# Eight weight buffers in SBUF, 1040 columns apart in place of 1024, the lower four moved by 4 columns

## The reference

```
mod = silu(c) @ w_ada + b_ada                 # 2048 x 12288, for 9 condition rows
h   = rmsnorm(x) * (1 + scale1) + shift1
qa, ka, va, qb, kb, vb, r, glr = split(h @ w_in)          # 2048 x 6160
x   = x + gate1 * (concat(attention, gated linear attention) @ w_out)   # 2048 x 2048
h2  = rmsnorm(x) * (1 + scale2) + shift2
g_pre, u = split(h2 @ w_up)                               # 2048 x 11264
x   = x + gate2 * ((silu(causal_conv(g_pre)) * u) @ w_down)             # 5632 x 2048
```

## Time and profile before

| what | value |
|---|---|
| time before, median of 3 runs | 1544.93 us (1543.18 to 1546.24) |
| profiled execution: span from first to last instruction | 1544.0 us |
| PE busy with matmuls | 1514.8 us, 98% of the span |
| PE loading stationary operands | 1372.8 us, 89% |
| DVE busy | 875.7 us, 57% |
| ACT busy | 633.9 us, 41% |
| matmuls of each of L989, L990, L991 | 3136 |

### The profile page before, as it was taken

One profiled execution on the slowest core, in us unless ns is written; L12 is line 12 of the kernel. 1 busy time (PEld: TensorE's weight loads), 2 busy tenths in 40 slices (PEclk: granted clock), 3 DMA queues, 4 the chain that ended last, 5 costly groups with the idle time before them and its releaser, 6 DMA issues.

```text
span 1544.0 us, 27862 instructions
## 1 busy us (share of the span) xinstructions
PE 1514.8 (98%) x11762; PEld 1372.8 (89%) x11762; DVE 875.7 (57%) x1509; ACT 633.9 (41%) x873; POOL 52.4 (3%) x89
## 2 busy tenths in 40 slices
PE   8999999999999889999999999999999999999999
PEld 4877888888888557768899999999999999999999
DVE  3655676666667435557454555555554565656574
ACT  3433444434445215235333333334333445545453
POOL 2000000001111000000000000000000000000000
PEclk8999999999999999999999999999999999999999
DMA  9998777777777997997644444454545444454541
GB/s 354 400 355 346 307 257 257 257 259 267 255 288 270 413 414 309 422 363 292 251 164 164 164 164 169 159 184 147 188 146 182 163 172 178 166 181 172 178 176 53
DMA packets 62283, 370.98 MB, mean 240 GB/s; under 512 B 7431, under 2 KB 7913, under 8 KB 27081
## 3 DMA queue, kind: packets, MB, share of 16 engines
q1 hardware_dynamic: 56096, 351.08, 60.6%
q0 software_dynamic: 5904, 17.93, 3.4%
q10 hardware_dynamic: 162, 0.22, 0.0%
HBM read 359.32 MB, written 9.88 MB: 239 GB/s over the span
## 4 chain that ended last, share of the span: by engine, by line
PE 89%; DMA 5%; DVE 3%; SPq 2%; ACT 1%; issue 1%; POOL 0%; ACTq 0%; DVEq 0%
PE ps L989 26%; PE ps L990 25%; PE ps L991 25%; PE ps L941 4%; PE ps L934 1%; SPq L710 1%; DMA ring<-in_w_ada_early 1%; DMA ring<-in_w_out 1%; DMA ring<-in_cache_k_win 1%; DMA proj<-in_tables 1%; ACT whi L1501 1%; DVE wlo L2028 1%; PE ps L1321 1%; DMA ring<-in_w_ada 1%; PE ps L1290 1%
## 5 line engine op out<-in xcount | busy, mean ns | idle before, releaser
L989 PE MATMUL ps<-hhi,whi 128*128 128x288 f32 x3136 | 934.0, 298 | 3.1 <-DVE wlo L1871 1.6
L990 PE MATMUL ps<-hlo,whi 128*128 128x288 f32 x3136 | 922.6, 294 | 0.0
L991 PE MATMUL ps<-hhi,wlo 128*128 128x288 f32 x3136 | 922.5, 294 | 0.0
L989 PEld LDWEIGHTS ps<-hhi,whi 128*128 128x128 f32 x3136 | 589.0, 188 | 38.8 <-issue 29.9
L990 PEld LDWEIGHTS ps<-hlo,whi 128*128 128x128 f32 x3136 | 589.2, 188 | 0.7
L991 PEld LDWEIGHTS ps<-hhi,wlo 128*128 128x128 f32 x3136 | 588.9, 188 | 0.0
L1492 ACT ACTIVATE whi<-ring 128x1024 fp32r<-128x1024 f32 x178 | 185.7, 1060 | 200.7 <-PE ps L991 200.7
L1864 DVE TENSOR_TENSOR wlo<-ring,whi 128x1024 fp32r<-128x1024 f32 x178 | 212.0, 1221 | 78.8 <-ACT whi L1492 78.4
L2028 DVE TENSOR_TENSOR wlo<-ring,whi 128x1024 fp32r<-128x1024 f32 x96 | 117.0, 1223 | 79.6 <-ACT whi L1501 79.5
L1501 ACT ACTIVATE whi<-ring 128x1024 fp32r<-128x1024 f32 x96 | 100.8, 1053 | 130.1 <-PE ps L991 114.2
L2545 DVE TENSOR_TENSOR wlo<-ring,whi 128x1024 fp32r<-128x1024 f32 (+1 forms) x94 | 105.7, 1132 | 56.2 <-ACT whi L1805 56.2
(11 more groups left out here) (298 smaller groups left out, 905.4 us busy)
## 6 DMA issues: line engine op xcount, KB each, us to landing
ring<-in_w_up SPq DMA_DIRECT2D x88, 1024.0 KB, 4.8
ring<-in_w_down SPq DMA_DIRECT2D x32, 1408.0 KB, 6.1
ring<-in_w_ada SPq DMA_DIRECT2D x42, 1024.0 KB, 6.8
ring<-in_w_in SPq DMA_DIRECT2D x28, 1024.0 KB, 6.5
ring<-in_w_ada_early SPq DMA_DIRECT2D x22, 1024.0 KB, 7.5
proj<-in_w_ada SPq DMA_DIRECT2D x22, 1024.0 KB, 11.0
ring<-in_w_in_early SPq DMA_DIRECT2D x20, 1024.0 KB, 9.3
ring<-in_w_out SPq DMA_DIRECT2D x16, 1024.0 KB, 13.2
```

The lines of the kernel that those rows point to most:

```text
L989: mm(out, w_hi, x_hi, start=start, stop=False)
L990: mm(out, w_hi, x_lo, start=False, stop=False)
L991: return mm(out, w_lo, x_hi, start=False, stop=stop)
```

## The change

The buffers of each part get a pitch of 1040 columns (4160 bytes). Buffer b of `whi` then begins 4160 b bytes after a multiple of 4096, which is 0, 64, 128 or 192 bytes past a multiple of 256. The buffers of `wlo` are moved by 4 columns (16 bytes) more: they begin 16, 80, 144 or 208 bytes past a multiple of 256. The four cache homes move along with buffers 2 and 3 of each part. Nothing stands behind these tensors, so nothing else moves. The instructions of every engine, their order, their waits and their sizes stay the same; addresses alone differ.

```diff
-BUFS, CHUNK = 4, 1024
+BUFS, CHUNK, PITCH = 4, 1024, 1040
...
             hhi = sbr("hhi", [P, KD, ROW], parts)[:, :, 0:TOK]
             hlo = sbr("hlo", [P, KD, ROW], parts)[:, :, 0:TOK]
-            whi = sbr("whi", [P, BUFS, CHUNK], parts)
-            wlo = sbr("wlo", [P, BUFS, CHUNK], parts)
+            whi = sbr("whi", [P, BUFS, PITCH], parts)[:, :, 0:CHUNK]
+            wlo = sbr("wlo", [P, BUFS, PITCH], parts)[:, :, 4:4 + CHUNK]
         rows_hi_lo = sb("rows_hi_lo", [P, 2 * KD * ROW])
-        weights_hi_lo = sb("weights_hi_lo", [P, 2 * BUFS * CHUNK])
+        weights_hi_lo = sb("weights_hi_lo", [P, 2 * BUFS * PITCH])
...
-        UNIT_AT += [(weights_hi_lo, c, 512) for c in (2048, 6144, 3072, 7168)]
+        UNIT_AT += [(weights_hi_lo, PITCH * b, 512) for b in (2, 6, 3, 7)]
```

## The result

The changed kernel takes 1548.13 us, the median of 17 runs, against 1543.41 us for 17 runs of the kernel before beside it: a ratio of 1.0025 [1.0018, 1.0032] (the bracket is the 95% interval; the ratio is worked out over all the runs and is not the quotient of the two medians). That is slower, by 2.8 to 4.9 us. The forecast was no change. The profiled execution took 1548.14 us, 1.6 us more than its span.

A forecast was written before the change was run, and what follows sets the result against it. PE was taken to bound the kernel, busy 98% of the span, with 9408 matmuls at 131.6 ns making 1238 of 1544.0 us. All terms were 0, so 1544.0 plus 0.93 us gave 1544.9 us, range 1536 to 1556.

The forecast's parts named there:

- The pace of PE: The 9408 matmuls of `three`, one every 131.6 ns: no change expected from the new addresses.
- Starting off the grid costs a load nothing there: Transposes at L1128 (8 bytes past a multiple of 16) and L1210 (aligned): both loads take 140 ns.
- their distance modulo 1024 changes from one matmul to the next, and the pace stays: Argument against block and row reads meeting by place: pace 131.5 to 131.7 ns through 23 and 33 matmuls.
- though not if the multiples of 256 alone decide: Exception left open: the pace could depend on block and row both beginning at multiples of 256 bytes.
- The first argument: Other engines' SBUF traffic does not disturb PE: 131.5 ns with DVE and ACT resting, 131.7 busy; cost nothing, bound 5.6 us.
- The bound of 10.3 us: Upper end for PE: each load of a shifted lower block takes 4 more columns, 3.3 ns x 3136.
- a wider step at L991 alone: Sign, beside longer loads, by which the slower rival would show: more time between matmul starts at L991 only.
- The conversions: ACT writing `whi`, DVE writing `wlo` at new places: cost nothing, bound 0.6 us either way.
- The cache units: Ten units of values and two of keys landing in moved buffers: cost nothing, bound +1.9 us.
- The sum: 1544.0 us of span plus four zeros, plus 0.93 us from span to median: 1544.9 us.
- The staggered starts let PE's two reads pass each other: Faster rival on PE: 109 us if all 11.6 ns goes; taken as 9.4 us, 1535.5 us; chance 0.21.
- The lower blocks begin off PE's reading grid: Slower rival: L991 loads fetch one group more, up to 3.3 ns, 1555.2 us; chance 0.21 with other worsenings.

The follow-up runs named there:

- pitch_1088: Changed kernel with a pitch of 1088 columns and no shift of `wlo`, so every block begins at a multiple of 256 bytes: 1544.0 us, ratio 0.9998 to before.
- shift_alone: Changed kernel with pitch 1088 in place of 1040: `whi` at multiples of 256 bytes, `wlo` 16 bytes past: 1548.93 us, ratio 1.0041 to before.
- pitch_alone: Changed kernel with its pitch of 1040 but without the 4-column shift of `wlo`: 1552.4 us, ratio 1.006 to before.
- pair_40: Changed kernel with pitch 1088 and all `whi` and `wlo` blocks 40 bytes past a multiple of 256: 1557.75 us, one execution.
- pair_168: Changed kernel with pitch 1088 and all `whi` and `wlo` blocks 168 bytes past a multiple of 256: 1533.37 us, ratio 0.9929 to before.
- all_moved: Changed kernel with pitch 1088 and both parts of rows and of weights 16 bytes past a multiple of 256: 1536.31 us, ratio 0.9955 to before.

## Why the prediction was wrong

- **The pace of PE** failed, at the step "Starting off the grid costs a load nothing there" and the "I take nothing" that follows from it. The term was taken as 0; it is 9408 x 0.44 ns = 4.1 us. The rows named for the step are not the right ones: `att_rows`, at 8 bytes, is the stationary of L1107, while L1128 turns parts of `proj` that begin at multiples of 128 bytes. The right row of the kernel before says the same:

```profile
L1107 PEld LDWEIGHTS ps<-con,proj 128*128 128x128 f32 x12 | 1.2, 141 | 1.6 <-ACT proj L1596 1.6
```

The starts say it too: in the short runs at L1107 and at L1210, behind their first distance, the matmuls start 109 ns apart at both. So the observation stands, and its transfer is what failed: these matmuls stream 128 columns, the ones of `three` 288, and there the pace does change with the place of the block, while the load of L991 stays at 188 ns. That the reads of block and row, which go on at the same time, interleave in another way is the likely reason, and no run shows it.
- In the same part, "their distance modulo 1024 changes from one matmul to the next, and the pace stays" was used against any dependence on place. (The distance of block and row changes only with every third matmul; the three of `three` have the same.) The sentence behind it named the exception, "though not if the multiples of 256 alone decide", and that is the case: pitch_1088 changes the address of every buffer but the first of `whi` and leaves the low 8 bits, and the time does not change.
- The first argument, that DVE, ACT and DMA do not disturb PE, was right, and it left out the place: where DVE and ACT both rest, the step of w_up is 133.1 ns in buffer 1 and 131.2 in buffer 3 after the change, and 131.7 and 131.6 before it. So the buffers differ without any work of the other engines.
- The bound of 10.3 us charged every third matmul, at 0.82 ns a column, worked out from loads of 32 columns (109 ns) and fp32r loads of 128 (188 ns); the plain float32 loads of 128 columns beside them, 140 ns, would give 0.32. The sign named for it, a wider step at L991 alone, did not come: after the change the steps behind L989, L990 and L991 rose by 0.4, 0.2 and 0.7 ns. shift_alone comes near this form, with most of its loss at one of three lines and loads no longer than before. But in pitch_alone all three lines lose (1.4, 0.5 and 0.9 ns) with every start at a multiple of 64 bytes, and pair_40 lost 13 us. That the bound held here is luck: its reason did not.
- **The conversions** were right: 1221 and 1059 ns, and the wait of ACT for PE in the trace grew with PE's time. The lines of the changed kernel that answer to the earlier trace rows, from 800 to 1500 us:

```profile
ACT whi L1492 <- PE ps L991: 173.0, 90, 2.4
DVE wlo L1864 <- ACT whi L1492: 62.7, 54, 2.3
```

- **The cache units** were right: the units in the moved homes land as before. The issues of the changed kernel that answer to the earlier trace rows:

```profile
rows_hi_lo<-in_cache_v_win SPq DMA_DIRECT2D x19, 512.0 KB, 15.3
weights_hi_lo<-in_cache_v_win SPq DMA_DIRECT2D x10, 512.0 KB, 14.3
ring<-in_cache_v_win SPq DMA_DIRECT2D x4, 512.0 KB, 15.6
weights_hi_lo<-in_cache_k_win SPq DMA_DIRECT2D x2, 512.0 KB, 13.7
```

14.3 and 13.7 us against 14.2 and 13.6, and the step of PE accounts for the whole loss within its interval. The bound of 1.9 us was not needed. By the Trainium skill (DMA: Bandwidth & Descriptors, section How a descriptor splits into AXI transactions), which speaks of reading, the prediction had put the estimate at 1546.8 us, if writing were alike; the 0.1 us between the medians does not show that cost.
- **The sum.** The 0.93 us added to the span came from two different executions; after the change one execution takes 1.6 us more than its own span. The median of before is 1543.41 us over 17 runs and not the 1544.9 of the first three. Neither touches the direction. The measured time lies within the range of 1536 to 1556 us, which the sizes of the two rivals had set.
- **The rivals.** "The staggered starts let PE's two reads pass each other" looked in the right place, at the address dependence of every matmul, and had the wrong sign for this change. With other places a gain comes out: pair_168 gains 11 us. That this is near the price of 9.4 us is luck, for the price stood for any one of the 11.6 ns. "The lower blocks begin off PE's reading grid" had the right sign; its mechanism, longer loads, did not show, and all_moved, where every block begins 16 bytes off, is faster than before. What the prediction's last paragraph named as its weak point, a pace that depends on the lowest 8 bits of the addresses, is what happened.

**What stays open.** Why a given pair of places allows 130.0, 131.67 or 133.3 ns and not another value, and what in the start of a run picks between two of them. No order of the table by distance, by sum or by period held. That the pace follows the places of block and row below 256 bytes, that a still row frees the step, and that some places have two paces, is shown; that the cause is two reads sharing one way into memory by turns is an argument from this, and was not shown. Rows were moved to one other place only, 16 bytes.

## What to carry to other kernels

In a stretch where PE never waits, count the starts per 100 us before touching the addresses of its operands: the pace here moves by -1.3 to +2.4%, and the mean durations tell less: between pair_168 and pair_40, whose steps are 130.0 and 133.3 ns, the matmuls of L990 go from 292 to 296 ns and their loads from 187 to 189. Low address bits of stationary and streaming operand are a tuning choice to be measured, with all buffers at one place so that the result can be read; a change that scatters the buffers over places gets about their mean, here worse than the one place that it left. An equal duration in small matmuls that come a few at a time, as the transposes here, does not carry over to another shape in a packed stream.

## What the runs showed of the hardware that was not expected

- The step of an fp32r matmul of 288 columns with a moving row lay between 130.0 and 134.9 ns as a buffer's mean, by the place of block and row below 256 bytes; with a still row it was 122.97 ns at the eight places of the changed kernel.
- The distances between starts form a pattern that repeats through thousands of matmuls: in before, 131, 131, 130 and 135 ns.
- For one and the same pair of places there can be two steady paces, 130.0 and 133.3 ns in pair_168, taken anew after each break of PE. Five timed runs of that kernel lay within 2.3 us, while a change of pace in its longest run would be 5663 x 3.3 ns = 19 us: from execution to execution the choice was the same in that run.
- A start 16 bytes off, for upper and lower blocks and rows alike, was better (130.77 ns) than the same kernel with everything at multiples of 256 bytes (131.67 ns).
